# Picking the tokens of experts 0 and 1 straight into feature-major form, in a two-layer encoder step on one core

## The reference, cut to what matters

```python
gate = jnp.sum(jax.nn.one_hot(e_idx, N_EXPERTS, dtype=jnp.float32) * w[..., None], axis=1).astype(x.dtype)
y = jnp.zeros_like(t)
for e in range(N_EXPERTS):
    h = jax.nn.silu(t @ w_gate[e]) * (t @ w_up[e])
    y = y + gate[:, e:e + 1] * (h @ w_down[e])
```

## Time and profile before

| what | value |
|---|---|
| runs shown | 906.44, 901.85 and 902.08 us |
| profiled execution | 906.25 us, of it the span of the trace 904.5 us |
| PE busy | 792.0 us (88%) |
| DVE busy | 333.7 us (37%) |
| ACT busy | 186.9 us (21%) |
| moved by DMA | 272.95 MB, mean 302 GB/s |

### The profile page before, as it was taken

How to read it: one execution, slowest core, us unless ns; L and a number is a source line. 1 busy time by engine, 2 the same in 40 slices (tenths; PEclk the granted TensorE clock), 3 DMA queues, 4 the chain that set the end, 5 groups by cost and what they waited for, 6 DMA issues and landing times.

```text
span 904.5 us, 9960 instructions
## 1 busy us (share of the span) xinstructions
PE 792.0 (88%) x3943; PEld 386.7 (43%) x3943; DVE 333.7 (37%) x749; ACT 186.9 (21%) x452; POOL 44.3 (5%) x59
## 2 busy tenths in 40 slices
PE   5998998989899877878899899989899999787785
PEld 3575777453433222222344667555434333222221
DVE  1115554544322221213270355563433343121148
ACT  1224334010311111110110135701004111111110
POOL 1202000003000000000200000000110000000020
PEclk9999999999999999999899999979799999899997
DMA  9822009466999999999898330680789999999991
GB/s 356 312 87 120 1 6 408 192 274 215 407 427 425 425 429 424 425 421 423 291 359 293 129 137 1 280 325 21 298 298 424 429 426 427 425 427 424 423 399 59
DMA packets 43744, 272.95 MB, mean 302 GB/s; under 512 B 6010, under 2 KB 10816, under 8 KB 25520
## 3 DMA queue, kind: packets, MB, share of 16 engines
q1 hardware_dynamic: 32608, 243.69, 65.6%
q0 software_dynamic: 5504, 20.09, 6.3%
q10 hardware_dynamic: 5584, 8.51, 2.6%
HBM read 255.35 MB, written 18.36 MB: 303 GB/s over the span
## 4 chain that ended last, share of the span: by engine, by line
PE 60%; DMA 25%; DVE 9%; ACT 2%; issue 2%; SPq 1%; ACTq 1%; POOL 0%; POOLq 0%; DVEq 0%
DMA arena<-in_expert_w_up 20%; PE bank L942 16%; PE bank L882 6%; PE bank L960 6%; PE bank L1208 4%; PE bank L1081 4%; PE bank L869 3%; PE bank L1129 2%; PE bank L856 2%; PE bank L969 2%; PE bank L801 2%; DMA arena<-in_w_mem_kv 2%; PE bank L703 1%; PE bank L849 1%; SPq L541 1%
## 5 line engine op out<-in xcount | busy, mean ns | idle before, releaser
L942 PE MATMUL bank<-arena 128*64 128x512 f32 x1024 | 237.4, 619 | 41.8 <-DMA arena<-in_expert_w_up 40.0
L942 PEld LDWEIGHTS bank<-arena 128*64 128x64 f32 x1024 | 76.4, 142 | 199.4 <-issue 145.2
L960 PE MATMUL bank<-arena 128*64 128x512 f32 x512 | 117.0, 599 | 16.6 <-DVE arena L1860 16.6
L1860 DVE COPY arena<-bank 128x256 f32<-128x256 f32 x32 | 13.5, 423 | 261.8 <-PE bank L951 261.8
L960 PEld LDWEIGHTS bank<-arena 128*64 128x64 f32 x512 | 33.8, 136 | 77.8 <-issue 54.2
L1410 ACT ACTIVATE arena<-bank 128x256 f32<-128x256 f32 x32 | 12.3, 383 | 256.0 <-PE bank L942 256.0
L1868 DVE RECIPROCAL arena<-arena 128x256 f32<-128x256 f32 x32 | 56.1, 1753 | 1.1
L882 PE MATMUL bank<-arena 128*128 128x512 f32 x128 | 56.0, 595 | 0.0
L1208 PE MATMUL bank<-arena 128*128 128x512 f32 x96 | 41.9, 594 | 2.3 <-DMA arena<-in_w_kv_shared 1.5
L1266 ACT COPY arena<-bank 128x512 f32<-128x512 f32 (+2 forms) x30 | 15.8, 536 | 110.6 <-PE bank L703 75.3
L1558 DVE COPY arena<-bank 128x512 f32<-128x512 f32 (+3 forms) x20 | 12.8, 648 | 68.7 <-PE bank L703 19.7
(11 more groups left out here) (273 smaller groups left out, 868.7 us busy)
## 6 DMA issues: line engine op xcount, KB each, us to landing
arena<-in_expert_w_down SPq DMA_DIRECT2D x64, 1024.0 KB, 28.1
arena<-in_expert_w_gate SPq DMA_DIRECT2D x30, 2048.0 KB, 18.8
arena<-in_expert_w_up SPq DMA_DIRECT2D x30, 2048.0 KB, 23.8
arena<-in_w_out SPq DMA_DIRECT2D x4, 2048.0 KB, 9.5
expert_rows<-arena ACTq DMA_DIRECT2D x60, 128.0 KB, 7.8
arena<-in_w_kv_shared SPq DMA_DIRECT2D x3, 2048.0 KB, 11.0
arena<-in_w_mem_kv SPq DMA_DIRECT2D x2, 2048.0 KB, 21.6
arena<-sorted_rows POOLq DMA_DIRECT2D x2, 2048.0 KB, 9.2
```

The costliest lines, as they stand in the source:

```text
L942: last = mm(bank[j][64 * half:64 * half + 64, :].rearrange("p (u f) -> p u f", u=2), slots[:, k, 0:CAP], w[:, :, k, 256 * half:256 * half ...
L960: last = mm(bank[3 + j][64 * n:64 * n + 64, :], hid_t[:, j, c, 64 * half:64 * half + 64], w[:, half, c, 512 * n:512 * n + 512], start=(hal ...
```

## The change: tokens stationary, one-hot moving

`pack_first` swaps the operands. For each block of 128 features (every eighth feature, as `xg` wants them) the tokens are now the stationary operand and the one-hot `pick` is the moving one, 128 columns wide. The product has features on the partitions and slots along the free axis, so it is what `xg` takes. There are 2 x 4 x 3 = 24 products of 128 columns in each layer in place of 6 of 512. The product of `keep_warm`, the eight transposes, `x_first`, the semaphore `first_turned` and one copy each on ACT and DVE are gone. The other copy of each stays, with the same shape, and reads bank 5 and bank 6.

```diff
         def first_dst(half):
             return (xg[:, :, 4 * half:4 * half + 4, :].rearrange("p j k s -> p k j s"),
-                    bank[(7, 5)[half]][:, :].rearrange("p (k j s) -> p k j s", k=4, j=2))
+                    bank[5 + half][:, :].rearrange("p (k j s) -> p k j s", k=4, j=2))
...
             def pack_first(l):
 
                 for half in range(2):
-                    for t, (a, n) in enumerate(TOKS):
-                        last = mm(bank[5 + half][:, :], pick[0:n, t, :], x_tok[0:n, t, 512 * half:512 * half + 512],
-                                  start=t == 0, stop=t == 2)
+                    for k in range(4):
+                        for t, (a, n) in enumerate(TOKS):
+                            last = mm(bank[5 + half][:, P * k:P * k + P], x_tok[0:n, t, 4 * half + k::KC], pick[0:n, t, :],
+                                      start=t == 0, stop=t == 2)
                     last.then_inc(packed, 1)
-                keep_warm(bank[1], 512)
-                for n, who in enumerate("av"):
-                    pe.wait_ge(first_taken[who], 2 * l + 1)
-                for half in range(2):
-                    b = bank[(7, 5)[half]]
-                    for k in range(4):
-                        last = tr(b[:, P * k:P * k + P], x_first[:, 4 * half + k::KC], ident)
-                    last.then_inc(first_turned, 1)
...
                     if e < 2:
                         for who in "av":
-                            pe.wait_ge(first_taken[who], 2 * (l + 1))
+                            pe.wait_ge(first_taken[who], l + 1)
...
                 ac.wait_ge(packed, 2 * l + 1)
-                nc.scalar.copy(x_first[:, 0:512], bank[5][:, :]).then_inc(first_taken["a"], 1)
-                ac.wait_ge(first_turned, 2 * l + 1)
                 nc.scalar.copy(*first_dst(0)).then_inc(first_taken["a"], 1)
...
                 ve.wait_ge(packed, 2 * l + 2)
-                V.tensor_copy(x_first[:, 512:D], bank[6][:, :]).then_inc(first_taken["v"], 1)
-                ve.wait_ge(first_turned, 2 * l + 2)
                 V.tensor_copy(*first_dst(1)).then_inc(first_taken["v"], 1)
```

More of the change, by code:

```diff
@@ L264, in encoder_step @@
         y_out = zr.cut(2, 512)
-        x_first = Region(y_at).cut(D)
         pair_t = zr.cut(NT)
@@ L310, in encoder_step @@
         tail_ready = sem("tail_ready")
-        packed = sem("packed"); first_turned = sem("first_turned")
+        packed = sem("packed")
         first_taken = {"a": sem("first_taken_act"), "v": sem("first_taken_dve")}
```

## The result

The changed kernel took 920.24 us (median of 4 runs, 918.59 to 925.33) against 901.97 us for the kernel before (4 runs, 899.63 to 906.44): a ratio of 1.0187, 95% interval 1.0155 to 1.0219. It is slower, by about 18 us, where 2 us of gain was forecast. The profiled execution took 921.22 us with a span of 919.4 us, 14.9 us more span than before (whose profiled execution was one of its long ones), and its mean granted clock was 0.932 where it had been 0.955.

The account below looks back on a forecast made before the run. The weight stream was taken to set the pace, its start waiting on PE's path; up products 1.86 us earlier a layer would gain 1.0 and 1.1, 2.1 us off 902.08, forecast 900.0 us, range 896.5 to 905.5 (own range 899.0 to 901.0).

Parts of the forecast that it names:

- The picking products: PE's products in `pack_first`: 48 records of 128 columns for 12 of 512, 5.23 to 5.40 us, +0.17 us a layer.
- three prices: Profile rows pricing a 128-column record: L801's products 0.112 us, transposes of `x_tok` 0.1125, transposes of `x_first` 0.121.
- The clock: PE's picking at 1.2 GHz: new records twice 0.1125 us at worst, 10.8 us, +0.5 us; nothing counted for losing `keep_warm`.
- The tail: From end of picking to first up product: 2.89 us falls to 0.86, so 2.03 us go in each layer.
- What reaches the end: Share of PE's 1.86 us earlier up products that shortens the run: 1.0 and 1.1 us in the layers, 2.1 in all.
- dip: Lower GB/s between the sorted rows' read and the weight plateau: 1.22 us lost in layer 0, 2.21 in layer 1.
- The line of 0.29 us for each us of distance: Dip's growth between the two layers' known points; gave the lower bound of 0.54 us gained a layer.
- distance: From issue of the sorted rows' read to expert 3's weight load: 5.16 and 8.60 us, forecast 3.30 and 6.74.
- The sorted rows: Read lands 9.2 us after issue, near 227; PE needs it at `turn_rows` about 232.5, so 5 us to lose.
- Loads that don't hide: Rival: load and pass add to 0.214 us a record, picking 10.3 us, run 908.1 us; chance 0.10.
- point of decision: Record time in the picking, 0.151 us, below which PE gains and above which the loads-that-don't-hide rival wins.
- Nothing reaches it: Rival: weights queue behind the sorted rows' read whenever issued, so no saving reaches the end, 902 us; chance 0.15.

Follow-up runs that it names:

- e2: Changed kernel with the tile of 32 rows padded to 128 with zeros of the one-hot, so no height changes; ratio 1.0032 to the kernel before.
- e6: Changed kernel with padded tiles and contiguous stationary tiles, weights of experts 0 and 1 loaded in matching feature order; ratio 1.0006 to the kernel before.
- e1: Changed kernel with the tiles in snake order, so the height changes 8 times and not 15; picking fell by 2.05 us.
- e5: Changed kernel with 12 dummy products instead of one right ahead of the picking, so it begins at full clock; picking 15.21 us.
- e4: Changed kernel with 128 adjacent features in the stationary tile in place of every eighth; picking 16.25 to 15.07 us.
- e8: Kernel before without the `keep_warm` dummy product between the picking and the transposes; ratio 0.9997.
- e3: Changed kernel with 3072 in place of 2048 dummy columns during the routing; PE's idle time behind them 2.13 to 0.41 us, clock fell just the same.
- e7: Kernel before with 3072 dummy columns in place of 512 behind the picking, a pure delay; ratio 1.0053, some 5 us slower.
- e9: e6 with the down products of expert 1 ahead of `turn_rows`; 907.53 us.
- e10: Kernel before with the down products of expert 1 ahead of `turn_rows`; median not below that of the kernel before.

## Why the prediction was wrong, step by step

**The picking products: the step that failed.** I priced a record at 0.1125 us and asked "are the loads really hidden?" The forecast was 5.40 us; it was 16.25, or 0.339 us a record. Each of the three prices came from a row that differs in something that mattered. L801's products have contiguous weights; the transposes of L703 and L978 read the same stride, but are transposes; none of the rows priced alternates in height, and all of them ran at full clock. "No row has a true product with a strided load" stood in the text, and the range for it went to +0.58 us only. The runs give the parts:

- stride: e2 against e6, 336 ns a load against 192, and 0.24 us a record against 0.112, also at full clock;
- tile height: e1 and e2, 0.29 and 0.30 us for each of 15 changes, 4.5 us in all (0.19 us each at full clock, e5);
- the clock: at 1.2 GHz a contiguous load is about as slow as a strided one (e4), and a contiguous record takes 0.213 us.

The parts therefore don't add. Without the stride alone it is 15.07 us, without the height changes alone 11.76, with full clock for its first third 15.21, and without stride and height changes 6.41.

The Trainium skill's rule that I set aside (TensorE: Matmul & The Clock Gate, "The mechanism": a load overlaps a running product only if their row groups differ) doesn't describe this either; the same section also lets a load into a background weight buffer run ahead, a case that the prediction left out and that no run here tells apart. In e6 loads on all 128 rows follow products on the same rows every 0.112 us, and it is the change from 128 rows to 32, a subset of them, that holds the next load back. To say "the trace does not agree" was right for L801 and too much for the case.

**The clock: mis-sized.** "The new ones twice 0.1125 at worst" made +0.5 us of a low clock. The picking at 1.2 GHz took 16.25 us, and it kept the clock low into the up products, +2.66 and +2.61 us, a term that I didn't have. In e5 the clock fell while this stream ran; in e1 and e4, with changes of height, it stayed low through the picking; in e2 and e6, without them, it rose during it.

**The tail: right.** 2.89 us became 0.87, so 2.02 went where 2.03 was forecast. Leaving `keep_warm` out of the kernel before left its time the same (e8), though the up products of one layer ran 1.46 us slower there.

**What reaches the end: the mechanism wrong in one direction.** I read the earlier trace rows by their GB/s and called the lack against 425 a dip that an earlier issue can fill. The DMA share stands in the same rows: 1.30, 1.16, 0.91 and 0.85 in layer 0. The engines were not idle there; they moved fewer bytes at that share. This holds for the start of the weights too: the read of 2,048 KB lands at 217.87 + 9.2 = 227.07, and the shares of 0.91 and 0.85 at 258 and 360 GB/s come after it. A packet counts in these rows where it starts, which is why a share can exceed 1. Spread over their durations, the packets of the trace fill each of the four stretches in layer 0 (1.0 of it), and 0.86, 0.34, 0.78 and 0.97 of those in layer 1. So in layer 0 the engines had no idle time to win, and in layer 1 about 1.1 us, where 1.22 and 2.21 us had been counted. The line of 0.29 us for each us of distance doesn't exist either. Between about 5 and 8 us of distance nothing is lost or won (5.21, 7.23, 7.87 and 7.99 us in e8 and e2 leave the stages within 0.6 us of before). Above that the loss is about one for one: taking the stage's growth from the distance leaves 6.8 to 7.7 us in layer 0 for the change, e1, e3, e4, e5 and e7. In layer 1 the stages of the same kernels grew by 0.9 to 1.1 us for each us of distance beyond the 8.60 of before, in e4 by 0.6. Distances below 5 us, in e6, e9 and e10, scatter from 3.1 us less to 2.3 us more, with one execution each. The change sits at 15.1, and 8.1 + 6.6 = 14.7 us of its 14.9 us of span are these two stages.

**The sorted rows: right for the change, wrong as a margin.** "It has 5 us to lose" counted the read of 2,048 KB alone. PE needs the one of 256 KB as well, which in the kernel before was issued at 218.66 and took 9.9 us, so the margin was about 4 us. Issued at 2.63 and 1.82 us of distance (e6), the weights stretch the large read from 9.2 to 14.5 and 16.7 us and the small one to 18.5 and 20.9, and PE waits 5.3 and 8.5 us. The Trainium skill says as much (DMA: Bandwidth & Descriptors, "Issuing engines are not separate DMA queues": transfers issued by different engines run on the same 16 and interleave), and the trace agrees: the reads took that much longer, while the engines together moved 353 and 355 GB/s, close to the 361 and 343 of before.

**The rivals.** Loads that don't hide was the right rival, at a chance of 0.10, and its point of decision, 0.151 us a record, held. Its price, 908.1 us, was 12 us short: 0.214 us a record where it was 0.339, with no clock in it. "Nothing reaches it" describes e6: with the picking near its forecast price the runs show no gain. The forecast's own 2.1 us would be a ratio of 0.9977, just outside e6's interval from 0.9980 to 1.0033. So they were most likely not there to be had, whatever the loads did; what the other order of the weights costs in e6 is the one part of this that no run separates.

What stays open: why a transpose with a stride is loaded at 193 ns (L978) and a product with the same stride at 336, and why the clock came back during the picking only in those kernels of 48 records that have no changes of height; nothing here tells. And no kernel here beats the one before by more than the runs can tell.

## What to carry to other kernels

Price a record by a row that agrees in kind of operation, stride of the stationary operand and rows in use; where no row agrees in all three, the upper bound is the load and the pass one after the other, at the lower clock if that may stand there, and not the nearest good row. Cutting wide moving operands into narrow ones multiplies the loads, and so lays bare whatever a load costs: keep the stationary operand contiguous and all tiles of one height, padded if need be. Before counting a dip in GB/s as time to win, read the DMA share in the same row; at 0.95 an earlier issue (e6) only slowed the transfer ahead of it. And look for every transfer that a wait stands for, the small one behind the large one too.

## What the runs showed of the hardware

- A load of a product's stationary tile of 128 x 128 f32 took 336 ns with every eighth element and 192 ns contiguous at 2.4 GHz (e2, e6); at 1.2 GHz 337 and 333 (e2, e4). The strided pace of 0.24 us a record was the same at both clocks; the contiguous one was 0.112 and 0.213 us (e6).
- Where the rows in use change between 128 and 32, the next load began 0.37 us after the start of the product ahead, and not 0.05 us (the change): 0.29 to 0.30 us for each change at 1.2 GHz (e1, e2), 0.19 at 2.4 GHz (e5).
- PE can lose full clock while its rows show it busy throughout: in e5 it fell in the midst of the picking, between 224 and 226 us, and between 681 and 683 us in layer 1.
- The read of 2,048 KB landed 9.2 us after its issue with the weights issued 5.16 us behind it, 14.5 us with 2.63, and 16.7 us with 1.82 (e6). The read of 256 KB behind it took 9.9, 18.5 and 20.9 us.
